# Projection stage of a hybrid decoder layer: result stores spread over two blocks, two small products on row groups, one sum of squares later

## The reference

```python
hn = rmsnorm(h, mix_norm[l])
a_q, a_f, a_i, a_g, b_y, b_x, c_u, d_z = jnp.split(hn @ w_in[l], IN_SPLITS, axis=-1)
...
zf = zf + mu.astype(F32) * (token_shift(zf) - zf)
r, k, v, w_lat, a_lat, g_lat = jnp.split(zf, RW_SPLITS, axis=-1)   # 32, 32 and 64 columns of latents
w = w0.astype(F32) + jnp.tanh(w_lat) @ w_up.astype(F32)            # decay
a = jax.nn.sigmoid(a0.astype(F32) + a_lat @ a_up.astype(F32))      # rate
g = jax.nn.sigmoid(g_lat) @ g_up.astype(F32)                       # gate
```

## Time and profile before

| what | value |
|---|---|
| median of 3 runs | 3237.93 us (3235.43 to 3238.3) |
| profiled execution | 3235.25 us, span 3233.5 us |
| mean granted TensorE clock | 0.975 |
| PE busy in the span | 3047.3 us (94%) |
| DVE, ACT, POOL busy | 2147.9, 1332.7, 497.1 us |
| first instruction of the scan stage on DVE | 578.17 us |
| DMA | mean 129 GB/s |

### The profile page before, as it was taken

How to read it: one execution, slowest core, us unless ns; L and a number is a source line. 1 busy time by engine, 2 the same in 40 slices (tenths; PEclk the granted TensorE clock), 3 DMA queues, 4 the chain that set the end, 5 groups by cost and what they waited for, 6 DMA issues and landing times. The chain is left out here.

```text
span 3233.5 us, 51255 instructions
## 1 busy us (share of the span) xinstructions
PE 3047.3 (94%) x20608; PEld 2508.9 (78%) x20608; DVE 2147.9 (66%) x3314; ACT 1332.7 (41%) x2125; POOL 497.1 (15%) x650
## 2 busy tenths in 40 slices
PE   8999999789989799989999889999899999999998
PEld 6778777688878578767888768888688887888887
DVE  6666565677748467544444577777877777787786
ACT  5656556455541322113233343333433333444443
POOL 4334333667640011100000000000000000000000
PEclk9999999899999899999999999999899999999999
DMA  6364564322210264330112333324332334876874
GB/s 212 101 221 132 181 205 125 102 68 75 68 35 5 99 223 164 112 117 33 65 59 71 111 110 107 110 104 139 116 111 105 117 112 132 272 216 216 254 219 125
DMA packets 200073, 416.20 MB, mean 129 GB/s; under 512 B 15281, under 2 KB 99505, under 8 KB 193457
## 3 DMA queue, kind: packets, MB, share of 16 engines
q1 hardware_dynamic: 199856, 413.18, 38.8%
HBM read 295.66 MB, written 117.46 MB: 128 GB/s over the span
## 5 line engine op out<-in xcount | busy, mean ns | idle before, releaser
L2975 PE MATMUL ffn_ps<-ffn_t_p,ffn_w_p 128*128 128x512 f32 x2640 | 606.1, 389 | 2.6 <-DVE ffn_w_p L3148 2.6
L2975 PEld LDWEIGHTS ffn_ps<-ffn_t_p,ffn_w_p 128*128 128x128 f32 x2640 | 495.4, 188 | 106.2 <-DVE ffn_w_p L3148 3.5
L2990 PE MATMUL ffn_ps<-ffn_t_p_parts 128*128 128x512 f32 x1416 | 329.3, 392 | 5.8 <-DVE ffn_t_p_parts L3290 5.8
L2990 PEld LDWEIGHTS ffn_ps<-ffn_t_p_parts 128*128 128x128 f32 x1416 | 267.8, 189 | 62.5 <-DVE ffn_t_p_parts L3290 6.6
L398 POOL TENSOR_TENSOR w_low<-w_ring,w_high 128x1024 fp32r<-128x1024 f32 x84 | 214.0, 2551 | 339.0 <-ACT w_high L548 339.0
L508 PE MATMUL proj<-hn_high,w_high 128*128 128x512 f32 x544 | 223.9, 420 | 2.6 <-ACT hn_high L538 1.6
L3001 ACT ACTIVATE ffn_w_p<-ffn_w_p_sums 128x512 fp32r<-128x512 f32 x132 | 83.4, 632 | 339.4 <-DVE ffn_w_p_sums L3169 339.2
L508 PE MATMUL proj<-hn_high,w_low 128*128 128x512 f32 x544 | 209.3, 393 | 0.0
L508 PE MATMUL proj<-hn_low,w_high 128*128 128x512 f32 x544 | 207.6, 390 | 0.0
L2990 PE MATMUL ffn_ps<-ffn_t_p 128*128 128x512 f32 x696 | 162.5, 389 | 0.0
L3071 ACT ACTIVATE ffn_t_p_parts<-ffn_ring 128x1536 fp32r<-128x1536 f32 x59 | 87.7, 1487 | 158.2 <-PE ffn_ps L2990 154.6
(11 more groups left out here) (519 smaller groups left out, 6678.6 us busy)
## 6 DMA issues: line engine op xcount, KB each, us to landing
ffn_ring<-in_w_up SPq DMA_DIRECT2D x44, 1024.0 KB, 5.5
ffn_ring<-in_w_down SPq DMA_DIRECT2D x88, 512.0 KB, 5.4
w_ring<-in_w_feat SPq DMA_DIRECT2D x84, 512.0 KB, 3.7
ffn_ring<-scratch_values SPq DMA_DIRECT2D x88, 257.0 KB, 4.6
scratch_gates<-ffn_gate SPq DMA_DIRECT2D x44, 512.0 KB, 2.6
ffn_ring<-scratch_gates SPq DMA_DIRECT2D x88, 256.0 KB, 3.8
scan_in<-scratch_scan SPq DMA_DIRECT2D x16, 896.0 KB, 4.5
scratch_values<-ffn_raw SPq DMA_DIRECT2D x22, 513.0 KB, 3.6
```

The source lines that it names most:

```text
L2975: mm = pe.matmul(bank(name, s), w_part(name, a)[:, k * P:(k + 1) * P], t_part(name, b)[:, k * TB:(k + 1) * TB], start=k == a == b == 0, st ...
L2990: mm = pe.matmul(ps[:, DOWN_BANKS[2 * t + c]], down_part(n, x)[:, HID + t * TC:HID + (t + 1) * TC], down_part(n, y)[:, c * DH:(c + 1) * DH ...
```

## The change

1. The stores of a block are split. The 13 whose results are finished early (`vd`, `csig`, `kk`, `b`, `kp`, `dg`, `bonus`) go out in the same block behind the loads 17 to 22 (loads 21 to 23 are the next block's 0 to 2). The other 12 (`va`, `cu`, `q`, `k`, `cum`, `ag`, `yb`) go out in the next block behind the loads 5 to 8, each with the wait for its own result.
2. The products of decay and rate take only the 32 rows that count (0 to 31 of the latents for the decay, 32 to 63 for the rate), and stand in pairs: decay and rate of feature tile 0 behind tile 6, those of tile 1 behind tile 7. ACT empties them in that order.
3. In the last block the sum of squares stands behind half of the last quarter of `tokens_across`: 12 matmuls later.

```diff
-            STORE = WR + 2
+            def store_early(p, n):
+
+                if n == 17:
+                    sp.wait_ge(*vaux_out.at(p, 1))
+                    tokens(p, "vd")
+                    sp.wait_ge(*csig_done.at(p))
+                    features(p, "csig")
+                if n == 18:
+                    sp.wait_ge(*rk_ready.at(p))
+                    features(p, "kk")
+                if n == 19:
+                    features(p, "b")
+                if n == 20:
+                    features(p, "kp")
+                if n == 21:
+                    sp.wait_ge(*aux_out.at(p, 5))
+                    features(p, "dg")
+                if n == 22:
+                    sp.wait_ge(*vaux_out.at(p, 5))
+                    features(p, "bonus")
+
+            def store_late(p, n):
+
+                if n == 5:
+                    sp.wait_ge(*tok_out.at(p))
+                    sp.wait_ge(*k_ready.at(p))
+                    tokens(p, "va")
+                    tokens(p, "cu")
+                    features(p, "q")
+                if n == 6:
+                    features(p, "k")
+                    sp.wait_ge(*cum_ready.at(p))
+                    features(p, "cum", (0,))
+                if n == 7:
+                    features(p, "cum", (1,))
+                    sp.wait_ge(*ag_ready.at(p))
+                    features(p, "ag")
+                if n == 8:
+                    sp.wait_ge(*dve_end.at(p))
+                    features(p, "yb")
...
                     sp.wait_ge(*w_split.at(p, n - WR))
                     load_w(n % NF)
-                    if has_before and n == STORE:
-                        sp.wait_ge(*dve_end.at(p - 1))
-                        sp.wait_ge(*tok_out.at(p - 1))
-                        sp.wait_ge(*k_ready.at(p - 1))
-                        left = list(results(p - 1))
-                    if has_before and STORE <= n < STORE + 5:
-                        store(left[(n - STORE) * 5:(n - STORE + 1) * 5])
+                    if has_next:
+                        store_early(p, n)
+                    if has_before:
+                        store_late(p - 1, n)
...
-                    if n in (6, 7, 8):
-                        for m in range(2 * (n - 6), 2 * (n - 5)):
-                            for_act(m, C["lora"][:, m], z[:, 0, 1:])
+                    if n in (6, 7):
+                        t = n - 6
+                        for part, rows in enumerate((slice(0, 32), slice(32, 64))):
+                            for_act(2 * t + part, C["lora"][rows, 2 * part + t], z[rows, 0, 1:])
+                    if n == 8:
+                        for t in range(G2):
+                            for_act(4 + t, C["lora"][:, 4 + t], z[:, 0, 1:])
...
+                        if (k, j) == (KT - 1, 1) and not has_next:
+                            sum_of_squares_b(p)
...
-                    if m == KT // 2 - 2 and not has_next:
-                        sum_of_squares_b(p)
...
                 for t in range(G2):
-                    take_small(t, T["decay"][:, t], ACT.Sigmoid, col("rw_w0", t))
-                take(7, bx[:, 0, LRU_TAPS - 1:])
-                for t in range(G2):
-                    take_small(2 + t, T["a"][:, t], ACT.Sigmoid, col("rw_a0", t))
-                take(8, bx[:, 1, LRU_TAPS - 1:])
+                    take_small(2 * t, T["decay"][:, t], ACT.Sigmoid, col("rw_w0", t))
+                    take_small(2 * t + 1, T["a"][:, t], ACT.Sigmoid, col("rw_a0", t))
+                    take(7 + t, bx[:, t, LRU_TAPS - 1:])
```

More of the change, by code:

```diff
@@ L292, in _ @@
             load_w(2)
[L294 to L303, removed]
@@ L305, in store, with features @@
-            def store(results):
-                for out, src in results:
-                    sp.dma_start(out, src).then_inc(stored.sem, 16)
-            def store_last(p):
-                at = bass.ds(p * CB, CB)
-                def features(part, name, src):
-                    for t in range(G2):
[L315 to L319, removed]
+            def features(p, name, ts=range(G2)):
+                part, names = ("scan", SCAN) if name in SCAN else ("late", LATE)
+                src = T["h" if name == "yb" else name]
+                for t in ts:
+                    sp.dma_start(D[part][bass.ds(p * CB, CB), :, names.index(name), t].rearrange("c p n -> p c n"),
+                                 src[:, t].rearrange("p (c n) -> p c n", c=CB)).then_inc(stored.sem, 16)
@@ new lines, in tokens @@
+            def tokens(p, name):
+                src = {"va": tok[:, :, 0:G2 * P], "cu": tok[:, :, G2 * P:], "vd": v_tok[:]}[name]
+                sp.dma_start(D[name][bass.ds(p * CB, CB)].rearrange("c p n -> p c n"), src).then_inc(stored.sem, 16)
+            def store_early(p, n):
[17 more added lines that the diff above has]
+                    features(p, "bonus")
@@ L321, in store_last @@
+            def store_last(p):
                 sp.wait_ge(*csig_done.at(p))
-                features("scan", "csig", T["csig"])
+                features(p, "csig")
                 sp.wait_ge(*rk_ready.at(p))
                 for name in ("kk", "b", "kp"):
-                    features("scan", name, T[name])
+                    features(p, name)
                 sp.wait_ge(*aux_out.at(p, 5))
-                features("late", "dg", T["dg"])
+                features(p, "dg")
                 sp.wait_ge(*vaux_out.at(p, 5))
-                features("late", "bonus", T["bonus"])
+                features(p, "bonus")
@@ L330, in store_last @@
                 sp.wait_ge(*proj_out.at(p, 14))
-                features("scan", "q", T["q"])
+                features(p, "q")
                 sp.wait_ge(*vaux_out.at(p, 1))
-                tokens("vd", v_tok[:])
+                tokens(p, "vd")
                 sp.wait_ge(*k_ready.at(p))
-                features("scan", "k", T["k"])
+                features(p, "k")
                 sp.wait_ge(*cum_ready.at(p))
-                features("scan", "cum", T["cum"])
+                features(p, "cum")
@@ L338, in store_last @@
                 sp.wait_ge(*ag_ready.at(p))
-                features("late", "ag", T["ag"])
+                features(p, "ag")
                 sp.wait_ge(*tok_out.at(p))
-                tokens("va", tok[:, :, 0:G2 * P])
-                tokens("cu", tok[:, :, G2 * P:])
+                tokens(p, "va")
+                tokens(p, "cu")
                 sp.wait_ge(*dve_end.at(p))
-                features("late", "yb", T["h"])
-            STORE = WR + 2
+                features(p, "yb")
             def run(p, has_next, has_before=True):
@@ L756, in run @@
                 for t in range(G2):
-                    dve.wait_ge(*aux_out.at(p, t))
+                    dve.wait_ge(*aux_out.at(p, 2 * t))
                     own.done(dve.tensor_tensor_scan(T["csig"][:, t], chunk_start, T["decay"][:, t], 0.0, ALU.mult, ALU.add),
@@ L769, in run @@
                     own.done(dve.scalar_tensor_tensor(T["kk"][:, t], k, col("rw_k_k", t), T["inv"][:, t], ALU.mult, ALU.mult))
-                    dve.wait_ge(*aux_out.at(p, 2 + t))
+                    dve.wait_ge(*aux_out.at(p, 2 * t + 1))
                     own.done(dve.tensor_tensor(T["b"][:, t], T["kk"][:, t], T["a"][:, t], ALU.mult))
```

## The result

| | before | after |
|---|---|---|
| median | 3237.34 us (4 runs, 3235.43 to 3238.3) | 3208.63 us (4 runs, 3205.94 to 3211.79) |
| ratio | | 0.9912, 95% interval 0.9899 to 0.9925 |
| span of the profiled execution | 3233.5 us | 3204.2 us |
| mean granted clock | 0.975 | 0.978 |

It is 28.7 us faster; the forecast was 28.1 us and a median of 3209.8.

The account below looks back on a forecast made before the run. PE was taken to be held in blocks 1 to 3 by SP's wait and store bursts making weight loads late. Stores 21.1, pairs 4.6 and sum of squares 2.4 gave 28.1 us off 3237.9: 3209.8 us, range 3202 to 3220.

Parts of the forecast that it names:

- What bounds the stage: PE between tiles 6 and 9: blocks 1 to 3 lose 4.49, 6.75 and 9.87 us against block 0, together 21.1.
- The stores, late part: 12 stores behind the next block's loads 5 to 8: blocks 1 to 3 take block 0's 22.50 us, gaining 21.1.
- the doubtful one: Last block's load 10: issued near 460 us, landing two or three us before ACT's need; rival still late, 9.87 lost, 0.10.
- SP's wait and store bursts: Start of the claimed chain in blocks 1 to 3: then late weight load, ACT's copy, ACT's emptying, PE; 21.1 us.
- The stores, early part: 13 stores behind loads 17 to 22 in blocks 0 to 2: cost nothing, 12.8 us between a load's issue and use.
- The rival on the other side: Early stores delay weight loads of tiles 17 to 23; gain gone at 14.2 us to land, 3274 at 16; chance 0.04.
- The pairs: Decay and rate products behind tiles 6 and 7 run two at once: 0.58 us a pair, eight pairs, 4.6 us.
- the change of form: PE switching between products on all rows and on 32 rows: 0.14 us each way, 0.28 a pair.
- The sum of squares: Last block, 12 matmuls go ahead and fill PE's idle time: stage ends 2.4 us earlier, bounds 0 and 2.9.
- the two last stores: End of the stage: issued in about 0.5 us instead of 1.05 to 1.31, landing in 2.3 to 2.8.
- The sum: Whole kernel: 21.1 + 4.6 + 2.4 = 28.1 us faster, a median of 3209.8 us; chance 0.65.

Follow-up runs that it names:

- run 1: Kernel before with only the stores split over two blocks, products and sum of squares as they were: 3217.57 us, ratio 0.9944, stage 548.77 us.
- run 4: Kernel before with all 25 stores still in the next block, only their order and waits changed: 3216.84 us, ratio 0.9941 against the kernel before.
- run 5: Changed kernel with SP's old wait for DVE's last result back ahead of the first late store: 3212.97 us, ratio 0.9926 against the kernel before.
- run 10: Changed kernel with all 25 stores in the next block, last results and their waits last: 3212.00 us, ratio 0.9923 against the kernel before.
- run 6: Changed kernel with both decays behind tile 6 and both rates behind tile 7, on the same rows: 3218.38 us, ratio 0.9948 against the kernel before.
- run 3: Kernel before with only the last sum of squares 12 matmuls later: 3235.16 us, ratio 0.9996, stage 565.22 us.
- run 7: Changed kernel with the gate's 64-row products as a third with each pair: 3213.71 us, ratio 0.9930 against the kernel before, stage 543.13 us.

## Why the prediction was right

**What bounds the stage** was read rightly from the stretches of the earlier trace rows. The loss against block 0 was put at 4.49 + 6.75 + 9.87 = 21.1 us, and run 1 gave exactly that back.

**The stores, late part.** The step that carried the sum, that blocks 1 to 3 would behave like block 0, held to 0.01 us in each block (run 1). Load 10 of the last block, the doubtful one, landed 7.5 us after its issue at 445.15, at 452.7. (Block 3 begins 13.8 us earlier than in the kernel before; on that kernel's times the issue lies at 458.9, where 460 was forecast.) ACT took it at 457.31:

```profile
457.31 1.06 ACT L574 ACTIVATE w_high<-w_ring 128x1024 fp32r<-128x1024 f32 x1
```

That is 4.6 us of cover, not the two or three I had estimated. The landing behind the chunks was as in the earlier trace rows; SP was a little earlier than I placed it.

The chain named as cause, "SP's wait and store bursts", was right as the two together, but the prediction did not see that half of the edit was superfluous. Runs 4, 5 and 10 show that moving the wait, or storing 13 results early, each alone takes away the whole stall.

**The stores, early part.** Cost nothing, as said: run 1, which has them and the old products, takes 108.52 us from tile 9 to the next block's tile 6 (81.56 to 190.08), against 108.51. The six weight loads between 231 and 265 us, among which the early stores of block 1 stand:

```profile
DMA to landing us min/median/max: 3.7/4.0/4.1
```

That is 0.4 more in the median than in the earlier trace rows, against 12.8 us between issue and use. (The longest landing from 140 to 300 us, 7.3 us, belongs to a load at 298.6, among the late stores that SP issues in the next block.) The rival on the other side needed 14.2.

**The pairs.** Forecast 0.58 each, 4.6 us in all. Measured: 1.10 a block less the 0.09 by which the next stretch got longer, so 0.50 each, 4.0 in all. The overlap was right (0.86 saved, run 6). The mis-sized term is the change of form: 0.28 from the earlier trace rows, 0.35 in run 6. By the rows it is 0.09 before the pair (189.48 to 189.80 is 0.32, against 0.23 for a matmul) and 0.30 in it and behind it (1.39 to tile 7's second matmul, against 0.86 + 0.23), 0.39 together, where the stretches give 0.35. The change into the form, which the prediction took to be as cheap as the way out of the earlier trace rows, is the likely part that it had too small; the pair's first pass is recorded at 0.69 us, the later ones at 0.59. The rule of the Trainium skill ("TensorEngine Tiling (Array Packing)", Tiling Modes) that a change of mode drains the TensorE fits the trace, which has a cost at each change; the 0.35 us is what these runs add.

**The sum of squares.** Forecast 2.4, measured 88.21 - 85.82 = 2.39 against the traced execution of the kernel before. That this is so close is luck in part: against the other executions with the old order it would be 0.8 to 3.6 (run 3). The product and its reader gained 0.37 (from the product's start to DVE's first instruction 2.15 instead of 2.52), where I had 0.5; the two last stores gave the rest, landing in 2.9 to 3.4 rather than the 2.3 to 2.8 of the earlier trace rows.

**The sum.** 21.1 + 4.0 + 2.4 = 27.5 for the stage, and 27.5 measured. The median came 28.7 lower. Both are 0.6 from the forecast's 28.1, on either side of it, and that is closer than the scatter of the last term (0.8 to 3.6) and of the rest of the span would let one expect: the mechanism was right, and that the two came out so near is in part chance.

## What to carry to other kernels

Cut a repeating program at the same two places of its bounding engine and compare lengths: an iteration that lacks the suspected work is the measure for the others, and here it gave three quarters of the forecast, to 0.01 us in each block. A queue that carries both loads and stores should wait for a result only directly ahead of its own store; a wait at the head of the stores did no harm here when 12 instead of 25 followed it, so try one remedy before building two. A single traced execution can flatter a forecast: the idle time ahead of the sum of squares was the same in four executions, and what it cost was not. Small products on different rows of the array cost one product for two, but group all of one form together, since a change of form cost 0.35 us where a pair saved 0.86, and a 64-row product did not run beside 32-row ones.

## What the runs showed of the hardware that was not expected

- Products of 32 rows and of 64 rows on rows that do not overlap ran one after the other: 1.05 us from the start of one to that of the other (run 7), where two of 32 rows start together.
- The rest of the program, the same code in every kernel here, took from 2647.2 us (changed kernel) to 2657.9 us (pairs only) in twelve profiled executions, on average at clocks that gave the whole span 0.978 and 0.973. This scatter of up to 11 us from one execution to the next is larger than any single effect in the stage but the stall, so such effects have to be read from the trace. It may also be why runs 5, 7 and 10, whose stages are within 0.2, 2.0 and 0.1 us of the changed kernel's, have medians 3.4 to 5.1 us above it: the rest of the span was 7.7, 7.3 and 1.7 us longer in their traced executions. One execution of each does not prove it for the medians. What makes the clock of the later stages fall more often in one execution than in another stays open.
- The same product behind the same 3.0 us of idle time took 1.99, 2.41, 3.49 and 3.78 us in four executions, with a granted clock of 1.00 in the first and 0.50 in the last.
